# Hybrid decoder block with hierarchical MoE: the rows of all expert blocks but the last pair are loaded and combined while that pair computes, and the last pair's gated rows are added by one-hot products

## The reference, cut to what matters

```python
gates = g_p * e_p / sum(e_p)                # two gates a token, top-2 experts of its top-1 group
# (token, expert) pairs are sorted by expert into blocks of one expert each, at most 128 rows a block
hdn = silu(xb @ w_gate[e]) * (xb @ w_up[e]) # each block: 1024 -> 512
ys  = hdn @ w_down[e]                       # 512 -> 1024
out = h + segment_sum(ys * gate, token)     # per token: its row of h plus two gated expert rows
```

## Time and profile before

| | us |
|---|---|
| median of 3 runs | 1252.49 |
| lowest and highest | 1252.26, 1253.56 |
| the profiled execution's own time | 1252.73 |
| its span in the trace | 1251.0 |
| TensorE busy in the span | 1127.7 (90%) |
| VectorE busy | 629.8 (50%) |
| ScalarE busy | 534.8 (43%) |
| GpSimd busy | 222.7 (18%) |

### The profile page before, as it was taken

One profiled execution on the slowest core, in us unless ns is written; L12 is line 12 of the kernel. 1 busy time (PEld: TensorE's weight loads), 2 busy tenths in 40 slices (PEclk: granted clock), 3 DMA queues, 4 the chain that ended last, 5 costly groups with the idle time before them and its releaser, 6 DMA issues.

```text
span 1251.0 us, 18120 instructions
## 1 busy us (share of the span) xinstructions
PE 1127.7 (90%) x6677; PEld 853.8 (68%) x6677; DVE 629.8 (50%) x909; ACT 534.8 (43%) x804; POOL 222.7 (18%) x256
## 2 busy tenths in 40 slices
PE   6999999999998999999887999998999998989960
PEld 5999988899995666666666886655555555556530
DVE  6422333234326566665478865555545544445526
ACT  7302141144335445444335864455544554444520
POOL 4000001130300111000132213222222222222110
PEclk9999999999999999999988999999999999999985
DMA  9420015324014332221278999999999999999869
GB/s 266 102 69 1 1 47 189 135 104 136 1 42 111 95 97 76 73 68 68 94 292 324 369 379 404 420 426 405 392 398 391 405 391 398 402 383 398 355 246 366
DMA packets 66250, 291.54 MB, mean 233 GB/s; under 512 B 10696, under 2 KB 36328, under 8 KB 53648
## 3 DMA queue, kind: packets, MB, share of 16 engines
q1 hardware_dynamic: 48176, 243.38, 51.2%
q0 software_dynamic: 16720, 42.65, 9.0%
q10 hardware_dynamic: 1296, 4.72, 1.0%
HBM read 270.62 MB, written 37.92 MB: 247 GB/s over the span
## 4 chain that ended last, share of the span: by engine, by line
PE 59%; DMA 21%; DVE 7%; issue 7%; ACT 4%; SPq 1%; POOL 0%; DVEq 0%; ACTq 0%; POOLq 0%
DMA wg<-in_w_gate 18%; PE ps L1027 10%; PE ps L1028 10%; PE ps L1029 10%; PE ps L1343 4%; PE ps L1345 3%; PE ps L1344 3%; PE ps L1154 3%; PE ps L1122 2%; PE ps L1136 2%; ACT wg_high L1689 2%; DMA y<-expert_rows 2%; PE ps L1357 2%; DVE probs L2102 1%; PE ps L1192 1%
## 5 line engine op out<-in xcount | busy, mean ns | idle before, releaser
L2154 DVE TENSOR_TENSOR wu_low<-wu,wu_high 128x2048 fp32r<-128x2048 f32 x36 | 81.1, 2287 | 54.9 <-ACT wu_high L1689 54.9
L1357 PE MATMUL ps<-wu,xa 128*64 128x512 f32 x224 | 102.1, 598 | 0.0
L1357 PE MATMUL ps<-wg,xa 128*64 128x512 f32 x224 | 102.1, 598 | 0.0
L1689 ACT ACTIVATE wd_high<-wd 128x2048 fp32r<-128x2048 f32 x36 | 66.9, 1906 | 80.6 <-DMA wd<-in_w_down 78.8
L2154 DVE TENSOR_TENSOR wd_low<-wd,wd_high 128x2048 fp32r<-128x2048 f32 x36 | 81.2, 2288 | 35.8 <-ACT wd_high L1689 35.6
L1689 ACT ACTIVATE wu_high<-wu 128x2048 fp32r<-128x2048 f32 x36 | 66.9, 1907 | 67.0 <-DMA wu<-in_w_up 67.0
L2154 DVE TENSOR_TENSOR wg_low<-wg,wg_high 128x2048 fp32r<-128x2048 f32 x36 | 81.0, 2289 | 21.6 <-ACT wg_high L1689 21.6
L2257 DVE TENSOR_TENSOR hid<-sil,ps 128x512 f32<-128x512 f32 x18 | 12.4, 686 | 131.4 <-PE ps L1345 131.4
L1689 ACT ACTIVATE wg_high<-wg 128x2048 fp32r<-128x2048 f32 x36 | 66.9, 1907 | 26.4 <-DMA wg<-in_w_gate 24.8
L967 POOL DMA_INDIRECT expert_rows<-yb,idxs x32 | 47.9, 1497 | 160.1 <-ACT yb L1738 121.8
L1027 PE MATMUL ps<-uh,w_high 128*128 128x342 f32 (+1 forms) x208 | 71.4, 343 | 0.0
(11 more groups left out here) (388 smaller groups left out, 2980.2 us busy)
## 6 DMA issues: line engine op xcount, KB each, us to landing
wg<-in_w_gate SPq DMA_DIRECT2D x32, 2048.0 KB
wu<-in_w_up SPq DMA_DIRECT2D x32, 2048.0 KB, 21.2
wd<-in_w_down SPq DMA_DIRECT2D x32, 2048.0 KB, 20.1
u_rows<-u POOLq DMA_DIRECT2D x16, 512.0 KB, 6.4
y<-expert_rows SPq DMA_DIRECT2D x16, 512.0 KB, 10.3
raw_c<-in_w_in SPq DMA_DIRECT2D x5, 1024.0 KB, 5.7
xin<-in_x SPq DMA_DIRECT2D x8, 512.0 KB, 9.9
zx<-in_x POOLq DMA_DIRECT2D x4, 1024.0 KB, 7.0
```

The lines of the kernel that those rows point to most:

```text
L1357: last = mm(ps[HALF * n:HALF * (n + 1), 7, :], xa[:, k, :], raw[m][:, 1, k, :], start=(k == 0), stop=(k == KT - 1))
L1689: A(flat_half(wh[m][:, :, :], n), flat_half(raw_kf(m, s), n), ACT.Copy).then_inc(w_high[m], 1)
L2154: return V.tensor_tensor(flat_half(wl[m][:, s, :, :], n), flat_half(raw_kf(m, s), n), flat_half(wh[m][:, :, :], n).bitcast(F32), ALU.subtr ...
```

## The change

1. SP loads h tiles 0 to 3 as soon as block 30's gate product has been made, ahead of block 31's down weights, into the place of freed weights. The y loads follow after `done_with["u"][0]` and `all_out`, tile by tile (y1 before y0); tiles 4 to 7 wait for block 31's gate and up products too, and their h rows are loaded there.
2. POOL takes the last pair's row numbers at the start, writes the gates to HBM, and near the end gathers the gates of the last pair's rows. It writes zeros to those rows in `expert_rows` (two indirect DMAs, up to 128 and 64 rows), and no longer scatters blocks 30 and 31. The two gathers of blocks that don't exist go. `all_out` now stands for the scatters of blocks up to 29 and the zeros.
3. The last pair's result stays on the chip: ACT multiplies it by its gates into a float32r high part, DVE makes the low part. DVE makes a 0/1 matrix (row of block x token) for each of the two blocks.
4. PE adds the rows to their tokens: for each tile of 128 tokens four products with the large block's rows (high and low, two halves), four with the small block's, and for tiles 4 to 7 (`BY_PRODUCT`) two float32 products with a diagonal matrix of gates that take y1's place in DVE.
5. DVE adds PSUM to the tile (`add_last`), and the tile goes out. For tiles 0 to 3 it still runs two scalar_tensor_tensor before, for tiles 4 to 7 one.
6. `down_half` of block 31 writes to banks 0 and 1, so it doesn't wait for block 30's result to be emptied.

```diff
@@ -423,21 +432,38 @@
...
+        end_slots = [l_(f"end_{m}_{n}", [P, NT // 2, D]) for m in "gu" for n in range(2)]
+        end_high = {m: Plan(nc, wh_at[m], conv_at)(f"end_{m}_high", [P, NT // 2, D]) for m in "gu"}
+        h1t = [end_slots[0], end_high["g"]]
+        y0 = [end_slots[2], end_slots[1]]
+        y1 = [end_high["u"], end_slots[3]]
+        e_ = Plan(nc, v_at - 4 * (2 * 2 * D), v_at)
+        large_rows = [e_(f"end_large_{n}", [P, D], F32R) for n in ("high", "low")]
+        small_rows = [e_(f"end_small_{n}", [P, F], F32R) for n in ("high", "low")]
+        x_plan = Plan(nc, xh2_at + 4 * KT * HALF, conv_at)
+        gate_diag = {t: x_plan(f"gate_diag_{t}", [P, P]) for t in BY_PRODUCT}
+        x_plan.at = xh2_at + 4 * KT * P
+        token_hot = [x_plan("end_hot_large", [P, T], F32R)]
+        token_no = x_plan("end_token_no", [P, T])
+        token_hot.append(x_plan("end_hot_small", [P, T], F32R))
+        def end_tile(pair, t):
...
@@ -760,19 +795,25 @@
+            def load_rows(pair, t, src):
+                sp.dma_start(end_tile(pair, t), src[P * t:P * (t + 1), :]).then_inc(tile_in[t + 1], 16)
+            sp.wait_ge(done_with["g"][0], last // 2 + 1)
+            sp.wait_ge(h1_out, 16 * NT)
+            for t in range(NT // 2):
+                load_rows(h1t, t, dram_h1)
             load_matrix("d", second, last, 1)
-            for s in range(2):
-                sp.wait_ge(done_with["g"][s], last // 2 + 1)
-            sp.wait_ge(h1_out, 16 * NT)
-            for t in range(NT):
-                sp.dma_start(h1t[:, t, :], dram_h1[P * t:P * (t + 1), :]).then_inc(y_in[t], 16)
+            sp.wait_ge(done_with["u"][0], last // 2 + 1)
             sp.wait_ge(all_out, 1)
             for t in range(NT):
-                for dst, src in ((y0, ys[P * t:P * (t + 1), :]),
-                                 (y1, ys[T + P * t:T + P * (t + 1), :])):
-                    sp.dma_start(dst[:, t, :], src).then_inc(y_in[t], 16)
+                if t == NT // 2:
+                    for m in "gu":
+                        sp.wait_ge(done_with[m][1], last // 2 + 1)
+                if t >= NT // 2:
+                    load_rows(h1t, t, dram_h1)
+                load_rows(y1, t, ys[T:, :])
+                load_rows(y0, t, ys[0:T, :])
@@ -981,20 +1022,59 @@
+            earlier = pool.value_load(plan[0:1, 3:4], min_val=1, max_val=LAST // 2)
+            def end_column(dst, src, n):
+                nc.gpsimd.tensor_copy(dst, src).then_inc(end_rows_ready, 1)
+                pool.wait_ge(end_rows_ready, n)
+                pool.sem_inc(pool_pass, 1)
+            end_column(end_rows[:, 0:1], column(last, scol), 1)
+            rows_of_small = column(last + 1, scol)
+            end_column(end_small[:, :], rows_of_small, 2)
+            for n in range(2):
+                end_column(end_rows[HALF * n:HALF * (n + 1), 1:2], rows_of_small[0:HALF, :], 3 + n)
+            nc.gpsimd.memset(end_gates[:], 0.0).then_inc(pool_step, 1)
+            count[0] += 1
+            pool.wait_ge(pool_step, count[0])
+            pool.wait_ge(gates_ready, 1)
+            pool.dma_start(dram_gates.rearrange("(p n) o -> p (n o)", p=P),
+                           gates[:, :, :].rearrange("p k t -> p (k t)")).then_inc(gates_out, 16)
             free_result(0, 1)
-            with pool.Fori(2, last, 2) as i:
+            with pool.Fori(2, last - 2, 2) as i:
                 for s in range(2):
                     free_result(1 - s, i // 2 + s)
+            pool.wait_ge(gates_out, 16)
+            pool.wait_ge(end_rows_ready, 5)
             for s in range(2):
-                scatter(last + s, s, 2 * last + 5 + s)
-                if s == 0:
-                    free_result(1, last // 2)
+                pool.sem_inc(pool_pass, 1)
+                nc.gpsimd.indirect_dma_start(
+                    out=end_gates[:, s:s + 1], out_offset=None, in_=dram_gates[:, :],
+                    in_offset=bass.IndirectOffsetOnAxis(ap=gate_at[:, s:s + 1].bitcast(U32), axis=0),
+                    bounds_check=last_row, oob_is_err=False).then_inc(end_gates_in, 16)
+            pool.wait_ge(x_turned, last + 1)
+            pool.sem_inc(pool_pass, 1)
+            nc.gpsimd.memset(xg[:, 0, :], 0.0).then_inc(pool_step, 1)
+            count[0] += 1
+            pool.wait_ge(pool_step, count[0])
+            for rows_ in (end_rows[:, 0:1], end_small[:, :]):
+                pool.sem_inc(pool_pass, 1)
+                nc.gpsimd.indirect_dma_start(
+                    out=ys[:, :], in_=xg[:, 0, :], in_offset=None,
+                    out_offset=bass.IndirectOffsetOnAxis(ap=rows_.bitcast(U32), axis=0),
+                    bounds_check=last_row, oob_is_err=False).then_inc(rows_zero, 16)
+            scatter(last - 2, 0, 2 * last + 1)
+            free_result(1, earlier)
+            nc.gpsimd.iota(token_no[:, :], pattern=[[1, T]], base=0, channel_multiplier=0,
+                           allow_small_or_imprecise_dtypes=True).then_inc(end_rows_ready, 1)
+            scatter(last - 1, 1, 2 * last + 2)
+            pool.wait_ge(rows_zero, 32)
             for s in range(2):
-                pool.wait_ge(ys_out[s], 16 * (last // 2 + 1))
-                pool.wait_ge(xg_in[s], 16 * (last // 2 + 2))
-            pool.wait_ge(h1_out, 16 * NT)
+                pool.wait_ge(ys_out[s], 16 * (last // 2))
             pool.sem_inc(all_out, 1)
@@ -1381,14 +1461,15 @@
-            def down_half(b):
+            def down_half(b, bank=5):
                 pe.wait_ge(h_taken, b + 2)
-                pe.wait_ge(y_taken, b + 1)
+                if bank == 5:
+                    pe.wait_ge(y_taken, b + 1)
                 pe.wait_ge(w_in_sems["d"][1], 8 * (b + 1))
                     for j in range(2):
-                        last = mm(ps[HALF * j:HALF * (j + 1), 5 + j, :], ha[:, k, :], wd[:, 1, k, 512 * j:512 * (j + 1)],
+                        last = mm(ps[HALF * j:HALF * (j + 1), bank + j, :], ha[:, k, :], wd[:, 1, k, 512 * j:512 * (j + 1)],
                                   start=(k == 0), stop=(k == FT - 1))
@@ -1434,7 +1515,46 @@
             turn_hidden(last + 1)
-            down_half(last + 1)
+            down_half(last + 1, 0)
+            def end_bank(t):
+                return (2, 5, 0)[t % 3]
+            def end_large(t):
+                if t >= 3:
+                    pe.wait_ge(fin_ready, t - 2)
+                if t in BY_PRODUCT:
+                    pe.wait_ge(tile_in[t + 1], 16 * 4)
+                    for j in range(2):
+                        mm(ps[:, end_bank(t) + j, :], gate_diag[t][:, :], end_tile(y1, t)[:, F * j:F * (j + 1)],
+                           start=True, stop=False)
+                for part in large_rows:
+                    for j in range(2):
+                        mm(ps[:, end_bank(t) + j, :], token_hot[0][:, P * t:P * (t + 1)], part[:, F * j:F * (j + 1)],
+                           start=(part is large_rows[0] and t not in BY_PRODUCT), stop=False)
+            def end_small_rows(t):
+                for part in small_rows:
+                    for j in range(2):
+                        half_rows = slice(HALF * j, HALF * (j + 1))
+                        last_mm = mm(ps[:, end_bank(t) + j, :], token_hot[1][half_rows, P * t:P * (t + 1)],
+                                     part[half_rows, :], start=False, stop=(part is small_rows[1]))
+                last_mm.then_inc(end_made, 1)
+            pe.wait_ge(diag_ready, 1)
+            pe.wait_ge(hot_ready, 2)
+            pe.wait_ge(y_taken, last + 2)
+            end_large(0)
+            end_large(1)
+            pe.wait_ge(y_taken, last + 3)
+            end_small_rows(0)
+            end_small_rows(1)
+            for t in range(2, NT):
+                end_large(t)
+                end_small_rows(t)
@@ -1784,12 +1904,23 @@
             silu_half(last + 1)
-            take_y(last // 2 + 1, last + 2, 0)
+            act.wait_ge(gates_ready, 1)
+            for t in BY_PRODUCT:
+                diag = A(gate_diag[t][:, :], ident[:, :], ACT.Copy, scale=gates[:, 1, t:t + 1])
+            diag.then_inc(diag_ready, 1)
             take_hidden(last + 1)
-            take_y_half(last + 1)
+            act.wait_ge(all_out, 1)
+            act.wait_ge(end_gates_in, 32)
+            act.wait_ge(done_with["d"][0], last // 2 + 1 + counted["d"][0])
+            A(large_rows[0][:, :], big[:, 5 * 512:7 * 512], ACT.Copy, scale=end_gates[:, 0:1]).then_inc(end_high_ready, 1)
+            act.wait_ge(done_with["d"][1], last // 2 + 1 + counted["d"][1])
+            for j in range(2):
+                half_rows = slice(HALF * j, HALF * (j + 1))
+                A(small_rows[0][half_rows, :], ps[half_rows, j, :], ACT.Copy,
+                  scale=end_gates[half_rows, 1:2]).then_inc(end_high_ready, 1)
             for t in range(NT):
                 act.wait_ge(fin_ready, t + 1)
-                act.dma_start(out[P * t:P * (t + 1), :], h1t[:, t, :]).then_inc(fin_out, 16)
```

(49 more changed lines are left out.)

38 lines of the change are left out of this document (29 added, 9 removed).

## The result

The changed kernel takes 1247.24 us (1245.17 to 1248.3) against 1253.56 (1252.26 to 1255.77) for the kernel before on the same chip: a ratio of 0.9948, 95% interval 0.9931 to 0.9964, or 6.3 us. The forecast was 1246.0. The profiled execution took 1248.3, the slowest of five and 2.1 above its span. The lines of after stand here in the order of rows 1 to 7 and 10.

What follows compares the result with a forecast made beforehand. The bound was the serial end, with y loads waiting for the last product. Loads from 1204.3 land by 1236.7, DVE ends at 1241.7, the output adds 3.06: span 1244.8, plus 1.5 gives 1246; range 1239 to 1251.

Steps and rivals of the forecast that it cites:

- Part 1: When y loads can start: block 29's scatter lands 1.1 us after the weights queued before it, giving 1204.3.
- T0: Moment of SP's first y load at the end: forecast 1204.3, 11.1 us earlier than 1215.39.
- Rival B: Block 29's scatter has a landing time of its own: first y load at 1198, time 1240; chance 0.20.
- my low bound: Earliest first y load: 1198, if the scatter has a time of its own of 8 to 11 us.
- Part 3: Loads after the first y load: 13.11 MB at 0.416 MB/us, 31.5 us plus 0.9 start; tile 7 landed at 1236.7.
- Part 2: Main pipeline: block 31's weights land at 1203.2, within cover; products end near 1210.5, at no cost.
- Part 4: DVE at the end: adds of 1.285 and 1.23 us, ending at 1241.7; last output takes 3.06 more.
- Part 5: PE's products for tiles 4 to 7: 2.7 us a tile at full clock, 5.3 at half; cost taken as 0.
- Rival C: PE is the bound, at half clock through the last four tiles: time 1250.3; chance 0.10.
- D: Scatters of zeros and blocks 28 and 29 land one behind another: first y load 1219, time 1261; chance 0.08.
- E: The change doesn't overlap: `all_out` comes with the products' end, about 1211; time 1250 to 1254; chance 0.05.

Runs made afterwards that it cites:

- before_early_h: The kernel before, with only the loads of h tiles 0 to 3 moved ahead of block 31's down weights: 1254.28 us, 1.0001 of before.
- second profile: The changed kernel run and profiled again, unaltered: 1247.73 us, 0.9953 of the kernel before.
- y_after_weights: The changed kernel with SP's first y load also waiting for block 31's down weights: 1251.34 us, 0.9981 of the kernel before.
- no_product_rows: The changed kernel with gated rows of tiles 4 to 7 added by VectorE instead of TensorE products: 1248.17 us, 0.9951 of the kernel before.
- zeros_twice: The changed kernel with both scatters of zeros issued a second time, into a tensor nothing reads: 1249.77 us, 0.9977 of the kernel before.

## Why the prediction was right, and where it wasn't

The sign, the size and the kind of limit (the y loads, with DVE waiting for the last) came out. But two terms were wrong by 6 and 7 us in opposite directions, so that 1247.2 lies so near 1246 is luck; alone, one error would have put the time at about 1240, the other at about 1253.

- **Part 1, T0: wrong by 5.9** (1204.3, measured 1198.38; again 1196.03). Its failed step is "so I count a scatter's landing as that of the weights queued before it plus 1.1". The weights landed at 1207.4 and the scatter at 1198.3. The two landings 1.1 apart in the earlier trace rows were no rule: with 2.10 MB more ahead of the weights (before_early_h) they are 7.0 apart the other way. Nor does the one of the Trainium skill that I leaned on (DMA: Bandwidth & Descriptors, "Queues, rings and completion order", on HWDGE ordering; the prediction names the section before it) say what I took from it: as I read it now, a semaphore write waits for the writes that its engine has taken up, not for what is still queued in another ring. No run here tests that reading; the traces show the scatter overtaking. Rival B's value for T0 was right, and my low bound was this case.
- The issue of that scatter, put at 1186.5, came at 1189.70, as `down_half` of block 29 took 5.38 us for 3.58: PE was idle for 1.3 of the five us from 1181, and the clock granted over them is 0.72 of 2.4 GHz, so for a part of them it was at 1.2. In the second profile, without that dip, the issue was at 1186.18, 0.78 behind its rows in `yb`, as in the first. (The timeline puts the 2.20 us before it down to the zeros' landing, but in the kernel this scatter waits for its rows alone, and the zeros are waited for behind it.) The iota took 1.02 (0.9 assumed).
- **Part 3, the loads after T0: wrong by 7.2** (32.4 us, measured 39.6). The sum counted all bytes at the mean rate of 16 engines, as if they end together. Twelve had landed their parts of tile 7 by 1226.7, the last at 1238.0. In bytes the sum was 0.7 MB short (13.8 moved, 13.1 counted; some of what was queued before T0 came behind it), 1.7 us at 0.416; the shares from 1228 to 1238 leave 4.8 us of the 16 engines' time unused. Part 1 says "I count by the laggards" and part 3 didn't. Rival B's 1240 failed on the same term. With the pause (y_after_weights) 13.1 MB took 34.2 us, near the sum.
- **Part 2, the products:** 1210.5 foreseen, 1214.2 measured, at no cost, as foreseen. Block 30's weights came at 1196.6, not near 1193.0 (1191.7 and 1.3 of zeros): 23.8 us from their issue where it had been 20.2. The h tiles don't do that (before_early_h); the zeros and gate gathers are what is left, and a second pair of zeros didn't add to it, so its size isn't explained.
- **Part 4, DVE:** prices right (1.28 and 1.22 for 1.285 and 1.23; 0.75 for each 0/1 matrix). It ended at 1242.9 (1241.7): 1.3 of it from the last landing. The rest of 3.3 behind it for 3.06.
- **Part 5, PE:** the clock right, 1.00 to the end in this profile, and the step too, 0.43. But a float32 product takes two of these steps (tile 7's two products are four records from 1238.11 to 1239.50), and the sum had one. A tile costs PE 3.5 us (tile 4's products start at 1225.66, tile 5's at 1229.16), not 2.7, and by doubling 7 at half clock (an estimate), not 5.3. PE's last product ends at 1241.66 and DVE takes its sum at 1241.70, right behind the add before: the mistake cost nothing, but the slack of 1.1 us that the sum had was gone, and for tile 7 PE stands on the chain. In the second profile of after a part of the last tile ran at half clock (1236 to 1238 at 0.82), and DVE waited 1.58 us for PE. Rival C didn't come. The Trainium skill (TensorE: Matmul & The Clock Gate, "HAM oscillation — how this bites in real kernels") tells of waits for DMA between bursts of products; the fall to 0.50 in no_product_rows, without harm to the time, came where PE waited for DVE (L2461), so it is no case of just that.
- **The chances:** rival C's 0.10 is said to lie half on either side of 1250 and is then counted as 0.04 and 0.06, a slip of 0.01.
- **Rivals D and E:** the scatter of block 29 didn't starve (8.6 us; 8.3 to 14.3 over these kernels), though zeros_twice goes in D's direction; and T0 is not tied to the products' end.

## What to carry to other kernels

When loads are moved into a gap, ask what the gap was for besides idling: here it let the late DMA engines catch up, and with it filled their backlog fell on the last tile. (Filling it paid all the same: the pause put back cost 4 us.) Sum a stretch of DMA by its slowest engine, which the spacing of the 16 increments of one load shows, and not by mean bytes per microsecond; where several loads share a semaphore, only its last increment tells of a landing. Before you compare moments of two profiles, count them from a common event ahead of the change. Where indirect transfers are mixed with large loads, see that the rows really filled are spread evenly over the partitions, half tiles too: that was worth 30 us here, five times the change itself.

## What the runs showed of the hardware that I had not expected

- An indirect scatter overtakes a load queued 2 us earlier on another engine's queue: 8.6 against 19.7 us to landing (after), and 7.0 against 18.9 for one queued 4.9 us earlier (before_early_h).
- How the rows of indirect transfers lie over the partitions sets the speed of the large loads: with 8% of the DMA share in indirect transfers, their placement alone moved the weights' queue from 132.9 to 139.7 and 141.8 MB in 360 us, and the kernel from 1247 to 1226 and 1217 us.
- The parts of one tile can land 11 us apart: 36 of the last tile's 48 increments had come by 1226.7, the last at 1238.0.
